# A Trainium2 encoder step: the four plain feed-forward tiles become 2x2 block products, with the norm's factor applied when gate and up are read out

## The chip, the cores and the metric

The kernel runs on one core of one Trainium2 chip. The metric is the device time of one execution in microseconds. The kernel before takes 2283.16 us (median of 3 runs, 2282.57 to 2283.98).

## What is computed

Two layers of an encoder step over 640 tokens (512 prompt, 128 sample) of width 1024, then a final norm. Each layer adds a mixer part (four branches, merged and multiplied with w_out) and then the feed-forward part, which alone the change touches:

```python
def swiglu(h, wg, wu, wd):
    return (jax.nn.silu(h @ wg) * (h @ wu)) @ wd

x = x + swiglu(rmsnorm(x, norm_ffn), w_ff_gate, w_ff_up, w_ff_down)
```

The inner width is 2816, that is 22 tiles of 128. rmsnorm(x, g) multiplies a token's row by one factor (1 over the root of the mean square) and each channel by a gain. The factor is one number per token, so it can also be put on after the product with a weight; but silu needs the scaled gate, and the up product needs the factor too.

## The kernel before, in words

Channels lie on the 128 partitions and tokens along the free axis, so x is 8 tiles of 128x640 f32. A product in full precision is made of three matmuls on a high and a low part: high x high, weight high x activation low, weight low x activation high. High parts are cast by ScalarE (ACT), low parts are a subtraction (value minus high) on GpSimd (POOL) or VectorE (DVE). A matmul moves 320 tokens, half of the 640.

The feed-forward part is written out in FF_FLOW (line 121) as a list of steps, and each engine walks that list in its own order.

- A unit (ff_unit, L1239) is one output tile: for each of its contraction tiles, three matmuls for each half of the tokens. A gate or up unit has 8 contraction tiles, so 48 matmuls.
- A quad (block_product, L1257) is two output tiles at once, as a 2x2 block product with seven products in place of eight (Strassen's scheme in Winograd's form). The blocks are: the two halves of the contraction, the two output tiles, and the two token halves. The seven right operands are named A11, S3, S2, A12, S1, A22, S4; four of the seven weight operands are sums, F_SUM1 to F_SUM4. A gate or up quad is 7 x 4 x 3 = 84 matmuls for a pair of tiles, where units would take 96. A down quad over three pairs of inner tiles is 7 x 3 x 3 = 63 matmuls, and four of them make the 8 output tiles.

Before, pairs 0 and 1 of the 11 pairs (PLAIN = 2, so 4 gate and 4 up tiles) are units, and pairs 2 to 10 are quads. Down goes in four parts: 8 units of 4 tiles (inner tiles 0 to 3), 4 quads over pairs 2 to 4, 4 quads over pairs 5 to 7, and 8 units of 6 tiles (16 to 21).

The units come first for a reason that can be seen in the code: they work on hu_hi and hu_lo, rows with the gain but without the norm's factor (ACT L1731, DVE hu_low L1946), so they can start as soon as the last tile of x is there. While they run, PE sums the squares (L797) and spreads the factor over partitions (L805), ACT and DVE make rstd from it (L1358, L1362, L1928, L1932), gate_out and up_out put the factor on (L2402, L2413), and DVE and ACT prepare the seven operands of the quads with the factor in them (act_block L2422, act_sum L2428, act_high L1756, act_low L2432). From the first quad on no factor is needed.

One gate quad v starts at weight operand number n = v.n. The ring of split weights has RING = 5 slots, so the operand n+5+i can be cast only when product i is done.

- ACT: after product 0 it copies QX to QY (L1788), casts operand n+5 (L1726); after product 1 it copies QW to QZ; after 2 it copies QY to QV and to u2; after 3 it takes silu of QX straight from PSUM (L1791); after 4 it copies QV to u4; then silu of the other three blocks as they come. With each product it casts one more operand. If the quad follows an up quad of a split pair, it casts the blocks of that pair's value (L1809).
- DVE, in this order: three sums of the weights of the next quad (L2380, L2383, L2385), low parts n+5 and n+6 (L2393), the four block sums of the pair before (L2487), the fourth weight sum (L2374), low part n+8, block lows (L2496), the sum QW + u4 (L2468), low part n+9, two block lows, QZ + u2, low part n+11, two block lows. In an up quad there are no follow-ups of a pair before, but four products of gate and up (L2535, L2546, L2558, L2560).
- GpSimd: nothing but low parts (L751). Operands 0 and 3 of a gate or up quad are its own, and 0, 3, 4 and 6 of a down quad (POOL_OPS), in the order of the operands.
- PE: product 2 waits for the first copy, product 4 for the third, product 6 for the fifth; product 0 of the next quad waits until QX is read, product 1 until QW is read. Every product waits for the low part of its weight operand.
- SP loads 512 KB for each half of a quad's weights into four buffers, as soon as the low parts made from that buffer are done.

The main loop that leads into the feed-forward part adds the w_out product to x (L2346), one tile in about 7 us, and for each tile makes the square (ACT L1344), the running sum of squares (add_square, DVE L1961) and hu_hi and hu_lo. The last 8 down units add to x (L2612), sum squares and, in the first layer, make the next layer's operand (ACT L1371, DVE L1951).

## Time and profile before

| what | value |
|---|---|
| median of 3 runs | 2283.16 us |
| lowest and highest run | 2282.57 and 2283.98 us |
| span of the profiled execution | 2280.9 us |
| time around its span (median less span) | 2.3 us |
| PE busy | 2236.0 us, 98%, 14942 matmuls |
| DVE busy | 1425.9 us, 63% |
| ACT busy | 921.1 us, 40% |
| POOL busy | 954.3 us, 42% |
| chain that ended last | PE 87%, DVE 11%, ACT 1% |

The time shown beside the span is that of the runs: the profiled execution's own time is not listed apart, and the span from its first to its last instruction is 2.3 us under the median. The feed-forward part is at 714 to 1144 us in the first layer and again near the end in the second. The mean clock granted to PE over the span is 0.996 of full speed.

### The profile page before, as it was taken

How to read it: one execution, taken by the hardware profiler on the slowest of the kernel's cores; microseconds unless marked ns; L12 is line 12 of the kernel's file. 1: busy time of each engine (PE TensorE's matmuls, PEld its weight loads, DVE VectorE, ACT ScalarE, POOL GpSimd, SP SyncE). 2: the span in 40 equal slices, each digit the busy share in tenths (PEclk: the TensorE clock that was granted, in tenths of full speed). 3: DMA queues.
4: the chain of work that ended last, by engine and by line, in shares of the span. 5: the costliest groups of instructions: out<-in, count | busy, mean ns of one | idle time of the engine just before them, and what ended most of it. 6: DMA issues, size and time to landing. Idle time of an engine off the chain costs nothing.

```text
span 2280.9 us, 40378 instructions
## 1 busy us (share of the span) xinstructions
PE 2236.0 (98%) x14942; PEld 2156.1 (95%) x14942; DVE 1425.9 (63%) x2650; ACT 921.1 (40%) x1886; POOL 954.3 (42%) x988
## 2 busy tenths in 40 slices
PE   8999999999999999999999999999999999999997
PEld 7998998888999999999999999988889999999997
DVE  7998554343235868887489975434432376788864
ACT  4115233445213446665420153334442144566652
POOL 5554454233565433232465444532336644232321
PEclk9999999999999999999999999999999999999998
DMA  5251121011232122222244411210112222222221
GB/s 202 95 181 63 49 73 61 28 42 42 80 106 100 52 96 77 97 81 89 62 139 147 128 54 56 75 51 33 43 42 93 106 93 66 89 89 79 98 79 60
DMA packets 76970, 187.90 MB, mean 82 GB/s; under 512 B 20080, under 2 KB 30928, under 8 KB 75792
## 3 DMA queue, kind: packets, MB, share of 16 engines
q1 hardware_dynamic: 69008, 165.64, 21.9%
q10 hardware_dynamic: 7808, 20.16, 2.6%
q8 instruction: 102, 1.67, 0.3%
q14 instruction: 52, 0.43, 0.1%
HBM read 173.47 MB, written 14.14 MB: 82 GB/s over the span
## 4 chain that ended last, share of the span: by engine, by line
PE 87%; DVE 11%; ACT 1%; issue 1%; DMA 0%; SPq 0%; DVEq 0%; ACTq 0%
PE gemm L778 39%; PE gemm L1257 22%; PE gemm L1239 10%; DVE side L2078 7%; PE side L1257 4%; PE side L1121 2%; PE side L1101 2%; PE side L1052 1%; PE side L884 1%; DVE prod L1987 1%; PE side L1108 1%; DVE h_lo L1941 1%; PE side L972 1%; PE side L1062 1%; PE side L1239 0%
## 5 line engine op out<-in xcount | busy, mean ns | idle before, releaser
L751 POOL TENSOR_TENSOR ring_lo<-w_raw,ring_hi 128x512 fp32r<-128x512 f32 (+2 forms) x232 | 286.0, 1236 | 564.6 <-ACT ring_hi L1726 564.6
L732 POOL CAST w_hi<-w_raw 128x384 fp32r<-128x384 f32 x376 | 223.0, 593 | 702.2 <-PE gemm L778 666.9
L734 POOL TENSOR_TENSOR w_lo<-w_raw,w_hi 128x384 fp32r<-128x384 f32 x376 | 449.7, 1196 | 30.1
L778 PE MATMUL gemm<-h_hi,w_hi 128*128 128x320 f32 x1616 | 406.0, 332 | 6.5 <-DVE h_lo L1941 4.6
L778 PE MATMUL gemm<-h_hi,w_lo 128*128 128x320 f32 x1616 | 368.9, 309 | 0.0
L778 PE MATMUL gemm<-h_lo,w_hi 128*128 128x320 f32 x1616 | 368.3, 309 | 0.0
L778 PEld LDWEIGHTS gemm<-h_hi,w_hi 128*128 128x128 f32 x1616 | 273.8, 189 | 37.9 <-issue 17.1
L778 PEld LDWEIGHTS gemm<-h_lo,w_hi 128*128 128x128 f32 x1616 | 270.6, 188 | 0.0
L778 PEld LDWEIGHTS gemm<-h_hi,w_lo 128*128 128x128 f32 x1616 | 270.4, 188 | 0.0
L1257 PE MATMUL gemm<-act_hi,ring_hi 128*128 128x320 f32 x864 | 267.0, 309 | 0.0
L1257 PE MATMUL gemm<-act_hi,ring_lo 128*128 128x320 f32 x864 | 267.0, 309 | 0.0
L1257 PE MATMUL gemm<-act_lo,ring_hi 128*128 128x320 f32 x864 | 266.9, 309 | 0.0
L1726 ACT ACTIVATE ring_hi<-w_raw 128x512 fp32r<-128x512 f32 (+2 forms) x304 | 172.9, 571 | 122.4 <-PE gemm L1239 65.5
L2078 DVE SCALAR_TENSOR_TENSOR side<-conv_prompt,vec,side 128x512 f32<-128x512 f32 x232 | 175.2, 755 | 0.0
L2173 DVE TENSOR_TENSOR prod<-gate,gemm 128x320 f32<-128x320 f32 x96 | 42.3, 483 | 207.4 <-PE gemm L778 207.4
L1257 PEld LDWEIGHTS gemm<-act_hi,ring_lo 128*128 128x128 f32 x864 | 162.4, 188 | 0.0
L1257 PEld LDWEIGHTS gemm<-act_lo,ring_hi 128*128 128x128 f32 x864 | 162.4, 188 | 0.0
L1257 PEld LDWEIGHTS gemm<-act_hi,ring_hi 128*128 128x128 f32 x864 | 162.3, 188 | 0.0
L778 PE MATMUL gemm<-o_hi,w_hi 128*128 128x320 f32 x512 | 125.5, 326 | 3.1 <-issue 3.1
L778 PE MATMUL gemm<-o_lo,w_hi 128*128 128x320 f32 x512 | 116.8, 309 | 0.0
L778 PE MATMUL gemm<-o_hi,w_lo 128*128 128x320 f32 x512 | 116.7, 309 | 0.0
L2393 DVE TENSOR_TENSOR ring_lo<-w_sum,ring_hi 128x512 fp32r<-128x512 f32 (+1 forms) x156 | 102.7, 659 | 16.7 <-ACT ring_hi L1726 15.5
(357 smaller groups left out, 4703.8 us busy)
## 6 DMA issues: line engine op xcount, KB each, us to landing
w_raw<-in_ws_ff SPq DMA_DIRECT2D x88, 512.0 KB, 3.2
w_raw<-in_ws_gate SPq DMA_DIRECT2D x64, 512.0 KB, 3.2
w_raw<-in_ws_in SPq DMA_DIRECT2D x44, 512.0 KB, 3.3
w_raw<-in_ws_proj SPq DMA_DIRECT2D x64, 256.0 KB, 2.6
w_raw<-in_ws_fq SPq DMA_DIRECT2D x32, 384.0 KB, 3.4
w_raw<-in_ws_out SPq DMA_DIRECT2D x16, 512.0 KB, 3.2
w_raw<-in_ws_fd SPq DMA_DIRECT2D x16, 384.0 KB, 3.0
x_park<-x ACTq DMA_DIRECT2D x2, 2560.0 KB, 13.1
```

The lines of the kernel that those rows point to most:

```text
L732: eng.tensor_copy(w_hi[s][:, cols], w_raw[s][:, cols]).then_inc(w_high.sem, 1)
L734: eng.tensor_tensor(w_lo[s][:, cols], w_raw[s][:, cols], w_hi[s][:, cols].bitcast(F32), ALU.subtract).then_inc(w_split.sem, 1)
L751: eng.tensor_tensor(lo, src, hi.bitcast(F32), ALU.subtract).then_inc(lo_pool.sem, 1)
L778: mm = eng.matmul(dst[:, hf, 0:HALF], w, r[k][:, cols] if r in (xu_hi, xu_lo) else r[:, k, cols], start=first and k == 0 and part == 0, st ...
L1101: eng.matmul(bank[:, 0:w], qh[h % 2][:, P * i:w], kh[h % 2][:, 0:w], start=True, stop=True)\
L1121: mm = eng.matmul(B[6][:, i * P:(i + 1) * P], v_tok[k][:, two], PT[i % 2][:, k * P:(k + 1) * P], start=(k == 0), stop=(k == i))
L1239: mm = eng.matmul(dst[hf], w[:, cut], r[:, cols], start=part == 0 and k == 0 and t == 0, stop=part == 1 and k == tiles - 1 and t == 2)
L1257: mm = eng.matmul(dst, w[:, cut], r, start=fresh and k == 0 and t == 0, stop=k == tiles - 1 and t == 2, skip_group_check=not fresh)
L1726: eng.activation(hi, src, ACT.Copy).then_inc(op_high.sem, 1)
L2078: eng.scalar_tensor_tensor(acc, src, w, acc, ALU.mult, ALU.add).then_inc(conv_step.sem, 1)
L2173: eng.tensor_tensor(t2[0][:, cols], sg[:, cols], G[1][:, hf, 0:HALF], ALU.mult)\
L2393: eng.tensor_tensor(lo, src, hi.bitcast(F32), ALU.subtract).then_inc(lo_dve.sem, 1)
```

## The change

All 11 pairs of gate and up become quads, on rows with the gain but without the factor, and down becomes quads for nine pairs (0 to 8). The last 8 units take 4 tiles (18 to 21). Tables and the order of work:

```diff
-PLAIN = 2
-FF_FLOW = (("gate", 2), ("up", 2), ("units", 0, 4), ("gate", 3), ("up", 3), ("gate", 4), ("up", 4),
-           ("gate", 5), ("downs", (2, 3, 4)), ("up", 5), ("gate", 6), ("up", 6), ("gate", 7), ("up", 7),
-           ("gate", 8), ("downs", (5, 6, 7)), ("up", 8), ("gate", 9), ("up", 9), ("gate", 10), ("up", 10),
-           ("units", 16, 6))
-SPLIT_PAIRS = (2, 3, 4, 5, 6, 7)
+FF_FLOW = (("gate", 0), ("up", 0), ("gate", 1), ("up", 1), ("gate", 2), ("up", 2),
+           ("gate", 3), ("downs", (0, 1, 2)), ("up", 3), ("gate", 4), ("up", 4), ("gate", 5), ("up", 5),
+           ("gate", 6), ("downs", (3, 4, 5)), ("up", 6), ("gate", 7), ("up", 7), ("gate", 8), ("up", 8),
+           ("gate", 9), ("downs", (6, 7, 8)), ("up", 9), ("gate", 10), ("up", 10), ("units", 18, 4))
+SPLIT_PAIRS = tuple(range(9))
```

GpSimd makes the low parts of the first five operands of the first quad, and in every gate quad it multiplies by rstd six times: each of the four gate blocks after silu (value), and the two blocks that are sums before silu (summed):

```diff
+                def quad(v):
+                    gate, pair = v.kind == "gate", v.pair
+                    def value(k, t, cols):
+                        eng.wait_ge(gate_act.sem, gate_act.at(l, 4 * pair + k))
+                        eng.tensor_tensor(gb[t][:, cols], gb[t][:, cols], rstd[:, cols], ALU.mult)\
+                           .then_inc(gate_done.sem, 1)
+                    def summed(k, t):
+                        eng.wait_ge(p_sum.sem, p_sum.at(l, 2 * v.index + k))
+                        eng.tensor_tensor(gb[t][:, hi_half], gb[t][:, hi_half], rstd[:, hi_half], ALU.mult)\
+                           .then_inc(gate_sum.sem, 1)
+                    for i in range(5, 10):
+                        operand_low(v.n + i)
+                    if gate:
+                        value(1, 0, lo_half)
+                        summed(1, 1)
+                        summed(2, 0)
+                    operand_low(v.n + 10)
+                    if gate:
+                        value(2, 1, hi_half)
+                    operand_low(v.n + 11)
+                    if gate:
+                        value(3, 0, hi_half)
+                        value(4, 1, lo_half)
```

DVE multiplies the other two blocks by rstd straight from PSUM:

```diff
+                    done(3)
...
-                    if up:
-                        done(3)
+                    if not up:
+                        eng.tensor_tensor(gb[0][:, lo_half], rstd[:, lo_half], QX, ALU.mult).then_inc(gate_raw.sem, 1)
+                    else:
...
+                    else:
+                        done(6)
+                        eng.tensor_tensor(gb[1][:, lo_half], rstd[:, lo_half], QV, ALU.mult).then_inc(gate_raw.sem, 1)
```

ACT takes silu later, and waits for GpSimd in between; the last two silus of a gate quad go into the next quad, or to the end of the gate quad where a down quad follows:

```diff
-                    if gate:
-                        silu_block(QX, gb[0][:, lo_half])
                     cast(n + 8)
...
                     copied(QV, u4)
+                    if gate:
+                        eng.wait_ge(gate_raw.sem, gate_raw.at(l, 2 * v.pair + 1))
+                        silu_block(gb[0][:, lo_half])
                     cast(n + 9)
...
                     done(5)
+                    cast(n + 10)
                     if gate:
-                        eng.wait_ge(p_sum.sem, p_sum.at(l, 2 * v.index + 1))
-                        silu_block(gb[1][:, hi_half], gb[1][:, hi_half])
+                        eng.wait_ge(gate_sum.sem, gate_sum.at(l, 2 * v.pair + 1))
+                        silu_block(gb[1][:, hi_half])
```

The operands of the quads are now made while the w_out product is added to x, tile by tile, in place of the full hu_hi and hu_lo: for tiles 0 to 3 A11 and S3; for tiles 4 to 7 S1, S2, S4 and A12 (which holds A22 too). The sums of the first quad's weights stand between, and the sum of squares and the factor come in the midst of the first quad:

```diff
+                for m in range(KT):
+                    eng.wait_ge(x_back[m // 4].sem, x_back[m // 4].at(l, 16))
+                    add_to_x(A_UNITS + 2 * M_PAIRS + m, m)
+                    act_sums(l, m)
+                    if m:
+                        add_square(l, 0, m - 1)
+                    for name in (A11, S3) if m < 4 else A_LOWS[:2] if m == 7 else A_LOWS:
+                        act_low(l, m, name)
+                    if m == 6:
+                        weight_sums(FF_QUADS[0], False)
+                weight_sums(FF_QUADS[0], True)
+                add_square(l, 0, KT - 1)
+                for name in A_LOWS[2:]:
+                    act_low(l, KT - 1, name)
+                operand_low(5)
+                operand_low(6)
                 row_factor(l, 1)
```

Here act_sums is one subtraction (S3) for tiles 0 to 3, and for tiles 4 to 7 three operations of 128x320 (S1, S2, S4). On PE, product 0 of the first quad waits for A11 alone, layer_norm_sum stands after product 3 and spread_factor after product 4. The signs of some sums are turned, without another operation. Buffers move, and the weights' bytes stay the same.

## Rows read from the trace of the kernel before

**Rows 1.** The page's part 1, its first line and the engines' busy time.

```profile
span 2280.9 us, 40378 instructions
PE 2236.0 (98%) x14942; PEld 2156.1 (95%) x14942; DVE 1425.9 (63%) x2650; ACT 921.1 (40%) x1886; POOL 954.3 (42%) x988
```

**Rows 2.** The timeline of ACT: copy of QX after product 0 of four quads.

```profile
828.65 0.42 ACT L1788 ACTIVATE gemm<-gemm 128x320 f32<-128x320 f32 x1 [1.13 <-PE gemm L1257]
...
853.29 0.42 ACT L1788 ACTIVATE gemm<-gemm 128x320 f32<-128x320 f32 x1 [1.08 <-PE gemm L1257]
...
865.61 0.42 ACT L1788 ACTIVATE gemm<-gemm 128x320 f32<-128x320 f32 x1 [0.44 <-PE gemm L1257]
```

**Rows 3.** Windows: gate with follow-ups, up, down quad: PE, PEld, DVE, ACT, POOL busy.

```profile
851.50:863.83 12.33, 12.33 (x86) 12.33 (x86) 11.79 (x21) 8.43 (x19) 2.57 (x3) 1.00 0.26 87
863.83:876.14 12.31, 12.31 (x86) 12.31 (x86) 9.33 (x17) 7.45 (x16) 2.94 (x3) 1.00 0.21 65
885.40:894.70 9.30, 9.30 (x65) 9.30 (x65) 8.68 (x15) 6.33 (x16) 4.16 (x4) 1.00 0.15 44
```

**Rows 4.** Timeline of GpSimd, low parts of three widths.

```profile
833.53 1.30 POOL L751 TENSOR_TENSOR ring_lo<-w_raw,ring_hi 128x512 fp32r<-128x512 f32 x1 [5.92 <-ACT ring_hi L1726]
...
882.71 1.02 POOL L751 TENSOR_TENSOR ring_lo<-w_raw,ring_hi 128x384 fp32r<-128x384 f32 x1 [6.24 <-ACT ring_hi L1726]
...
1101.95 0.74 POOL L751 TENSOR_TENSOR ring_lo<-w_raw,ring_hi 128x256 fp32r<-128x256 f32 x1 [1.95 <-ACT ring_hi L1726]
```

**Rows 5.** Timelines of GpSimd and DVE around 858 us.

```profile
858.17 1.57 POOL L751 TENSOR_TENSOR ring_lo<-w_raw,ring_hi 128x512 fp32r<-128x512 f32 x1 [6.34 <-ACT ring_hi L1726]
...
858.10 0.49 DVE L2487 TENSOR_TENSOR f_block<-square,f_block 128x320 f32<-128x320 f32 x1
858.51 1.79 DVE L2374 TENSOR_TENSOR w_sum<-w_raw,w_sum 128x512 f32<-128x512 f32 x1
...
869.88 0.68 DVE L2374 TENSOR_TENSOR w_sum<-w_raw,w_sum 128x512 f32<-128x512 f32 x1
```

**Rows 6.** The same timelines around 863 us, and DVE's idle time after it.

```profile
863.17 1.33 POOL L751 TENSOR_TENSOR ring_lo<-w_raw,ring_hi 128x512 fp32r<-128x512 f32 x1 [3.42 <-ACT ring_hi L1726]
...
863.26 0.48 DVE L2468 TENSOR_TENSOR gate<-side,square 128x320 f32<-128x320 f32 x1
865.20 0.69 DVE L2393 TENSOR_TENSOR ring_lo<-w_raw,ring_hi 128x512 fp32r<-128x512 f32 x1 [1.45 <-ACT ring_hi L1726]
```

**Rows 7.** DVE's timeline in the up quad that began at 863.83: low part 5, product.

```profile
868.67 0.68 DVE L2393 TENSOR_TENSOR ring_lo<-w_sum,ring_hi 128x512 fp32r<-128x512 f32 x1
...
870.89 0.49 DVE L2535 TENSOR_TENSOR prod<-gate,gemm 128x320 f32<-128x320 f32 x1 [0.33 <-PE gemm L1257]
```

**Rows 8.** DVE's timeline at the last tile of x and the factor.

```profile
714.82 0.89 DVE L2346 TENSOR_TENSOR x<-gemm,x 128x320 f32<-128x320 f32 x2 [4.62 <-PE gemm L778]
...
716.41 0.82 DVE L1961 TENSOR_TENSOR gate<-gate,square 128x640 f32<-128x640 f32 x1
...
718.03 1.92 DVE L1961 TENSOR_TENSOR gate<-gate,square 128x640 f32<-128x640 f32 x1
723.15 0.19 DVE L1928 RECIPROCAL rstd_tokens<-rstd_tokens 128x5 f32<-128x5 f32 x1 [3.19 <-ACT rstd_tokens L1358]
723.37 0.90 DVE L1932 TENSOR_TENSOR prod<-ident,rstd_tokens 128x384 f32<-128x384 f32 x2
```

**Rows 9.** Timelines where the last units begin: PE, ACT, DVE.

```profile
1097.73 0.46 PE L1239 MATMUL side<-f_hi,ring_hi 128*128 128x320 f32 x2
...
1099.15 0.72 ACT L1752 ACTIVATE hu_hi<-square 128x640 fp32r<-128x640 f32 x1
...
1099.27 1.40 DVE L2418 TENSOR_TENSOR hu_lo<-prod,hu_hi 128x640 fp32r<-128x640 f32 x1 [0.85 <-ACT hu_hi L1752]
1100.60 0.81 DVE L2418 TENSOR_TENSOR hu_lo<-square,hu_hi 128x640 fp32r<-128x640 f32 x1
...
1119.86 1.88 DVE L1961 TENSOR_TENSOR gate<-gate,square 128x640 f32<-128x640 f32 x1
```

More of the change, by code:

```diff
@@ L173, in unit @@
         units.append(len(ops))
-        first = min(4, (tiles + 1) // 2) if tiles < 6 else 4
+        first = tiles // 2
         add(len(loads) - 1, 0, first * P, True)
@@ L183, in quad @@
                                                    (a, HW, F_SUM1), (a + 1, 0, F_SUM4), (a + 1, HW, None))):
-            add(load, start, cols, i in POOL_OPS[q.kind], summed, q)
-    for _ in range(4 * PLAIN):
-        unit(KT)
+            add(load, start, cols, i in by_pool, summed, q)
     q = d = 0
-    last, units_since = None, len(units)
+    last = None
     for step in FF_FLOW:
@@ L201, in _ff_operands @@
                 unit(step[2])
-            units_since = len(units)
         for v in new:
-            v.g, v.before, v.units = len(quads), last, units_since
-            if last is not None and not units_since:
+            v.g, v.before = len(quads), last
+            if last is not None:
                 last.after = v
-            last, units_since = v, 0
+            last = v
             quad(v)
@@ L2368, in split_before @@
                     def split_before(k):
-                        eng.wait_ge(lo_dve.sem, lo_dve.at(l, FF_OPS[v.before.n + k].count if v.before else 0))
+                        if v.before and not FF_OPS[v.before.n + k].pool:
+                            eng.wait_ge(lo_dve.sem, lo_dve.at(l, FF_OPS[v.before.n + k].count))
                     if fourth:
@@ L2511, in quad @@
                     split = up and pair in SPLIT_PAIRS
[L2512 removed]
+                    follows = b is not None and b.kind == "up" and b.pair in SPLIT_PAIRS
                     def done(i):
```

485 lines of the change are left out of this document (224 added, 261 removed).

## The prediction

> **What bounds the kernel now.** I read the page first: PE is busy 2236.0 of 2280.9 us [rows 1], so what is taken from PE is worth its time, as long as nothing else becomes late. Then PE's waits: inside the quads there are none, and the feed-forward part has almost none. So the trace holds no stall that the change could remove; it can only shorten PE's work. Then the windows of one quad each. A gate quad with follow-ups lasts 12.33 us and DVE is busy 11.79 us of it; an up quad has 9.33 of 12.31; a down quad 8.68 of 9.30 [rows 3]. DVE stands close behind PE. Its spare time over a pair is 24.64 - 21.12 = 3.5 us. ACT (15.9 us in a pair) and GpSimd (5.5) have room. Last, the timelines of DVE and GpSimd side by side, since the change gives GpSimd new work.
>
> **PE's work.** Quads start 12.32 us apart (853.29 to 865.61, and 24.64 us for two from 828.65) [rows 2], which is 12.32 / 84 = 0.1467 us a matmul. Four gate and up pairs of tiles a layer turn from 96 matmuls into 84: 48 fewer. Down was 8 x 24 + 8 x 63 + 8 x 36 = 984 matmuls and is 12 x 63 + 8 x 24 = 948: 36 fewer. That is 84 a layer, 168 in all, 168 x 0.1467 = **24.6 us saved**. The bytes of weights are the same.
>
> **DVE's own work.** Two multiplications from PSUM in each gate quad, 0.48 us each as its like in [rows 6], so DVE's pair goes from 21.1 to 22.1 us of 24.64. The spare time shrinks to 2.5 us. Removed with the units are gate_out, up_out, act_block and act_low, all beside PE.
>
> **GpSimd's work and what it does to DVE.** GpSimd gets six multiplications of 128x320 with both inputs in SBUF in each gate quad. The trace has no such instruction. Low parts take 0.74, 1.02 and 1.30 us for 256, 384 and 512 columns [rows 4]; between the first two, 320 columns are 0.88 us. Bounds: 0.74 below and 1.02 above. GpSimd's pair becomes 5.5 + 5.3 = 10.8 us, still under half.
>
> The price is on DVE. At 858 us a low part on GpSimd ran for 1.57 us in place of 1.30, as DVE had begun a sum just before it, and DVE's next sum, two inputs in SBUF, took 1.79 us where the same one alone takes 0.68 [rows 5]: it ended 0.56 us after GpSimd did. At 863 us DVE read PSUM beside the same GpSimd instruction and took its usual 0.48 [rows 6]. So the two exclude each other when DVE has both inputs in SBUF, about 1.1 us for 512 columns and, by width, 0.7 to 0.75 for 320. Now GpSimd's low parts mostly fall where DVE waits or reads PSUM, and DVE's quads have room for that.
>
> I lay a pair out from the start of the gate quad, with DVE's order of the trace. The QX multiplication comes at 8.7, ACT's silu at 9.6 (after the copy to u4), GpSimd's value 1 at 10.1. DVE's QW sum is there at 10.6; summed 1 runs to 12.2 and holds up low part n+9 or the block lows by 0.7. The QZ sum comes at 13.4, so summed 2 at 13.6 to 14.3; it blocks n+11 by 0.45. Behind it stand low part n+10, which fell on DVE's idle 1.45 us before [rows 6] and now blocks it for 1.15, then value 2, 3, 4. DVE has from here nothing but sums and low parts with two SBUF inputs until 19 us, so each of the three blocks it by 0.73, and as DVE is late the next quad's low part 7 falls in too, 1.15. In all 0.25 + 0.7 + 0.45 + 1.15 + 3 x 0.73 + 1.15 and 0.4 for the up quad's own n+10 = 6.3 us of blocking a pair. DVE would need 22.1 + 6.3 = 28.4 us where PE needs 24.64. That is 3.8 us a pair by which DVE sets the pace.
>
> Where PE first feels it: low part n+5 of the up quad was ready at 868.67 + 0.68 - 863.83 = 5.5 us into the quad [rows 7] and is needed at 5 x 1.76 = 8.8. It has 3.3 us to spare and would come 4.6 later in a first pair, 7 later in the next: stalls of 1.3, then some 3.6 for each pair.
>
> The other end is given by the down quads: there GpSimd is busy 4.16 us and DVE 8.68, of which by my count of its 15 instructions about 6.6 is its own work; half of GpSimd's time blocks. With half of 5.3 a pair needs 22.1 + 2.65 = 24.8 us, PE's 24.64: no stall to speak of. This is the low bound (0.1 a pair) against 3.8. I take 2.9 for a pair, nearer the layout, since in it GpSimd's operations follow right on DVE's results and fall into its densest stretch.
>
> A gate quad before a down quad is dearer: a down quad's product takes 1.32 us, so its operands are due sooner, four low parts are GpSimd's, and values 2 to 4 stand between them. Bounds 1 and 4.5 us; I take 3.5. DVE enters about 1.8 us late at no cost, once for each run of quads between two relaxed stretches. A layer has three such runs, each of two pairs and one gate quad before down: 2 x 2.9 + 3.5 - 1.8 = 7.5 us (bounds 1 and 10). Pair 0 has no follow-ups in its gate quad but begins late: 1.5. Pair 10 has none either: 0. Sum a layer 3 x 7.5 + 1.5 = 24.
>
> The Trainium skill's page "SBUF — State Buffer", section "Who interferes with whom", says that a DVE instruction with two SBUF inputs and a GpSimd instruction that reads SBUF block each other fully, whoever issues first, and one with at most one SBUF input doesn't. By that rule every GpSimd operation in the dense stretch costs DVE its whole length, and the sum would be the layout's 3.8 a pair, not the half that the down quads show. Rows 5 and 6 agree with it (1.79 against 0.68 and 0.48 us).
>
> **The start of the feed-forward part.** Before, DVE had 4.62 us idle ahead of the last tile of x [rows 8] and PE went on at once with units. Now for tiles 4 to 7 DVE does the addition (0.8), three sums (1.5), squares (0.8), four low parts (2.0): 5.1 us of 7.04 and at tile 6 three weight sums (2.1) more, with GpSimd's five low parts (1.3 each) of the first operands falling in the same place. So it comes to the last tile 1 to 2 us late. S2 of tile 7 is due 3.5 + 1.3 = 4.8 us after the last unit; the chain is addition, ACT's gained half 0.4, S1, S2, S4 1.5, squares 0.8 (1.92 if blocked [rows 8]), low part 0.4: 4.0, plus lateness 1 to 2, plus up to two blockings of 1.1. Behind it stand A12, the fourth sum, the squares that layer_norm_sum needs, S1, S4, two operand low parts, then reciprocal and spreading (1.1 [rows 8]) before spread_factor after product 4. Lower bound 1.5, upper 6; I take 3.5 a layer.
>
> **The end.** In the last units tiles 20 and 21 now come 1.76 us after the start, not 3.52. Units began at 1097.73, the low part of tile 20 was done at 1100.67 [rows 9], so PE waits 1.2 us, bounds 0.7 and 2. Units take 3.52 us in place of 5.28; DVE's addition, squares and next operand are 0.81 + 0.73 + 0.8 = 2.4, with one blocking as at 1119.86 (1.88 us) [rows 9] 3.5. It just fits; 0 to 1 us in the first layer. I take 1.5 a layer together.
>
> **Sum.** -24.6 + 2 x (24 + 3.5 + 1.5) = -24.6 + 58 = +33 us on the span of 2280.9, so 2314 with 2.3 us around it; it stands on the median in the same way, 2283.2 + 33 = 2316. I round the terms down once for the doubt in the blocked share and give **2312 us**.
>
> **Rivals.** A difference of 0.2%, 4.6 us, is about what a measurement of this kernel can tell from none.
>
> 1. *DVE and GpSimd take turns, DVE sets the pace* (the forecast, other side of rival 2): 2290 to 2350. For: rows 3 and 5. The point from which it decides: blocking over 2.5 us a pair. Chance 0.52.
> 2. *The blocking is hidden as in the down quads.* Pairs stall 0 to 0.7 us, start and end cost 5 a layer, gates before down 1.5: -24.6 + 10 + 9 = -6, 2277; if the start fits too, -24.6 + 8 = -17, 2266. For: GpSimd is half idle and half of its time was free before. Against: DVE's 11.79 of 12.33. Chance 0.33, of it 0.26 under 2278.6.
> 3. *ACT waits in line for GpSimd.* gate_sum holds ACT until summed 1 is done, and behind it stand the cast n+11 and the copy of QX for the next quad, which product 2 needs at 15.8. If GpSimd's operations are 1.0 us or more, the copy comes 1 to 2 us late in each of 22 gate quads: +33, less 24.6, with start and end 2301. Against: about 1.5 us of slack in the layout. Chance 0.12.
> 4. *The change doesn't do what it says*, fewer matmuls gained than 168: 0.03.
>
> Faster 0.27, same 0.08, slower 0.65. The range, 2266 to 2346, leaves out the upper bound of all terms and the best of rival 2.
>
> **What would show it.** PE x14774, its busy time hardly smaller as waits appear at L1257 with DVE L2393 (ring_lo) as releaser, 1 to 4 us each, above all in the fifth product of up quads and the first of down quads. DVE's windows of a pair near 27 to 28 us and full; sums (L2380, L2383, L2374) with means well over 0.68. GpSimd's multiplication at 0.9 to 1.6 us. DVE's share in the chain of waits above 11%. Wrong if windows of a pair stay at 24.64 and PE waits only at the start; then the blocking was hidden. If the releaser is ACT's copy, rival 3.

## The result, and the profile after

The changed kernel takes 2328.44 us (median of 4 runs, 2327.0 to 2329.11) against 2283.19 (2282.57 to 2283.98) of the kernel before: ratio 1.0193, 95% interval 1.0179 to 1.0208. It is slower by 45 us, as forecast in sign and cause (2312, range 2266 to 2346), and 16 us slower than the forecast.

First the page, its span, busy times and the shares of the chain of waits:

```profile
span 2326.5 us, 40875 instructions
PE 2231.4 (96%) x14774; PEld 2137.5 (92%) x14774; DVE 1633.7 (70%) x2888; ACT 989.9 (43%) x2078; POOL 1093.9 (47%) x1110
...
PE 62%; DVE 32%; issue 4%; ACT 2%; DVEq 0%; POOL 0%; DMA 0%; SPq 0%; ACTq 0%
```

Against [rows 1] PE has its 168 matmuls less, but only 4.6 us less busy time; DVE is busy 208 us longer for 238 instructions more, which is 0.87 us for each: too much for two multiplications of 0.48 and some low parts. So DVE's old instructions have become longer. DVE's share of the chain is 32%.

PE's waits (engine, line, what it waited for: sum in us, times, longest) name the place:

```profile
PE side L1320 <- DVE ring_lo L2482: 32.0, 23, 2.5
PE gemm L1320 <- ACT gemm L1798: 8.5, 8, 1.4
...
PE gemm L1320 <- issue: 3.7, 2, 1.8
```

Inside the quads the kernel before had no such wait. The releaser of most is DVE's low part of a weight operand. ("issue" is time for which the view finds no releaser.) The pace of a run is read, as in [rows 2], from ACT's copy of QX, here of gate 2, gate 3 and the first down quad behind it:

```profile
778.90 0.42 ACT L1798 ACTIVATE gemm<-gemm 128x320 f32<-128x320 f32 x1 [1.08 <-PE gemm L1320]
...
806.77 0.42 ACT L1798 ACTIVATE gemm<-gemm 128x320 f32<-128x320 f32 x1 [1.08 <-PE gemm L1320]
...
821.07 0.42 ACT L1798 ACTIVATE gemm<-gemm 128x320 f32<-128x320 f32 x1
```

A pair takes 27.87 us where PE needs 24.64. The windows of the gate and the up quad of pair 2 (columns as in [rows 3]) show DVE full:

```profile
777.11:790.18 13.07, 12.85 (x87) 12.58 (x87) 12.83 (x22) 8.55 (x18) 3.34 (x4) 1.00 0.25 80
790.18:804.98 14.80, 12.31 (x85) 12.05 (x84) 14.63 (x19) 8.02 (x17) 9.54 (x8) 1.00 0.18 54
```

DVE is busy 27.46 of 27.87 us; without GpSimd's multiplications it is 22.07 (run 3 below), so 5.4 us of a pair are blocking, where the prediction's layout had 6.3. The timelines of DVE and GpSimd in pair 1 show what fills it (start, duration):

```profile
764.62 1.19 DVE L2482 TENSOR_TENSOR ring_lo<-w_raw,ring_hi 128x512 fp32r<-128x512 f32 x1
765.74 2.67 DVE L2539 TENSOR_TENSOR f_block_lo<-f_block,f_block_hi 128x320 fp32r<-128x320 f32 x2
768.33 1.36 DVE L2469 TENSOR_TENSOR w_sum<-w_raw,w_raw 128x512 f32<-128x512 f32 x1
769.73 1.25 DVE L2472 TENSOR_TENSOR w_sum<-w_sum,w_raw 128x512 f32<-128x512 f32 x1
771.02 1.64 DVE L2474 TENSOR_TENSOR w_raw<-w_raw 128x512 f32<-128x512 f32 x1
...
764.38 0.88 POOL L787 TENSOR_TENSOR gate<-gate,rstd 128x320 f32<-128x320 f32 x1 [1.23 <-DVE gate L2511]
765.22 1.75 POOL L773 TENSOR_TENSOR ring_lo<-w_raw,ring_hi 128x512 fp32r<-128x512 f32 x1
766.93 1.13 POOL L782 TENSOR_TENSOR prod<-prod,rstd 128x320 f32<-128x320 f32 x1
768.02 1.12 POOL L782 TENSOR_TENSOR gate<-gate,rstd 128x320 f32<-128x320 f32 x1
769.11 1.33 POOL L782 TENSOR_TENSOR prod<-prod,rstd 128x320 f32<-128x320 f32 x1
770.39 1.71 POOL L773 TENSOR_TENSOR ring_lo<-w_raw,ring_hi 128x512 fp32r<-128x512 f32 x1
```

GpSimd has no gap for 7.7 us, and each of DVE's instructions takes about twice its time (a sum of 512 columns 0.68 alone [rows 5], here 1.25 to 1.64): the two take turns here, instruction by instruction, as at 858 us in [rows 5]. That happens where the prediction's layout put it, from the sum QW + u4 to the next quad's low part 7. The multiplication alone takes 0.88 us, as estimated from the widths of [rows 4].

In a gate quad before a down quad a second wait shows, on ACT (in brackets: idle time before, and who ended it) and then on PE:

```profile
820.33 0.47 ACT L1838 ACTIVATE gate<-gate 128x320 f32<-128x320 f32 x1 [1.22 <-POOL gate L787]
...
821.53 0.41 PE L1320 MATMUL gemm<-f_block_hi,ring_hi 128*128 128x320 f32 x1 [1.43 <-ACT gemm L1798]
```

This is rival 3, in this one place only: ACT stands in line for GpSimd's "summed 2", and the copy of QX for the next quad behind it comes late (at 821.07, shown above).

The start of the feed-forward part has four gaps on PE, and DVE, which had 4.62 us idle before the last tile of x [rows 8], now comes to it without a gap, at 718.61 us. PE's last w_out matmul ended at 715.64 (714.71 before), so DVE is 3.0 us behind it where it was 0.1:

```profile
716.49 0.41 PE L1320 MATMUL gemm<-hu_hi,ring_hi 128*128 128x320 f32 x1 [0.70 <-POOL ring_lo L773]
...
721.18 0.41 PE L1320 MATMUL gemm<-s_hi,ring_hi 128*128 128x320 f32 x1 [0.90 <-ACT gemm L1798]
...
723.80 0.42 PE L1320 MATMUL gemm<-s_hi,ring_hi 128*128 128x320 f32 x1 [1.03 <-DVE s_lo L2043]
...
729.10 0.39 PE L1320 MATMUL gemm<-s_hi,ring_hi 128*128 128x320 f32 x1 [1.83 <-issue]
...
717.02 1.67 DVE L2474 TENSOR_TENSOR w_raw<-w_raw 128x512 f32<-128x512 f32 x1
718.61 0.88 DVE L2443 TENSOR_TENSOR x<-gemm,x 128x320 f32<-128x320 f32 x2
...
724.46 0.68 DVE L2463 TENSOR_TENSOR w_sum<-w_raw,first_sum 128x512 f32<-128x512 f32 x1
...
727.20 0.68 DVE L2482 TENSOR_TENSOR ring_lo<-w_raw,ring_hi 128x512 fp32r<-128x512 f32 x1
...
728.37 2.48 DVE L1993 TENSOR_TENSOR prod<-ident,rstd_tokens 128x384 f32<-128x384 f32 x2
...
724.47 6.10 POOL L773 TENSOR_TENSOR ring_lo<-w_raw,ring_hi 128x512 fp32r<-128x512 f32 x2 [3.39 <-ACT ring_hi L1793]
```

The diagonals for the factor took 0.90 before [rows 8], 2.48 now beside GpSimd's low parts. PE's largest gap, the 1.83 of "issue", stands ahead of product 4 and so ahead of the spreading; the diagonals end at 730.85, after PE goes on. What ends 0.1 us before PE goes on is the first of GpSimd's two low parts, that of operand 4: it runs from 724.47 to 729.00, 4.53 us where 1.30 is usual. From 724.46 to 727.88 DVE runs six instructions with two SBUF inputs one right behind the other, each in its usual time (0.68 for a sum), and GpSimd ends 1.1 us after the last. So here it was GpSimd that was held up, and not in turns. The same 6.1 us for the two low parts stand at the second layer's start and in run 3. When the two alternate and when one is held for several instructions, no run here shows.

The granted clock stays at 1.00 through this start, but not through the same start of the second layer: it has the same four gaps, and the windows of 4 us from 1872 and 1876 show 0.84 and 0.73. Quad 0 lasts 18.37 us there, against 17.41 in the first layer.

The last units start with one gap of 0.39 us, and the next layer's sum of squares in layer 0 follows with another. The rows are PE's sum of squares in the timeline of the kernel before, the same in the changed one, and the changed kernel's windows around it:

```profile
1143.84 1.25 PE L797 MATMUL side<-ones,gate 128*128 128x1 f32 x10 [0.17 <-issue]
```

```profile
1166.58 1.25 PE L860 MATMUL side<-ones,gate 128*128 128x1 f32 x10 [1.30 <-issue]
```

```profile
1164.00:1168.00 4.00, 2.70 (x21) 2.47 (x20) 3.74 (x3) 1.73 (x4) 3.84 (x4) 1.00 0.99 390
1168.00:1172.00 4.00, 4.00 (x19) 4.00 (x18) 1.61 (x3) 0.22 (x1) 2.35 (x3) 0.57 0.78 302
```

After PE's wait the granted clock is 0.57 for 4 us (for the most part the 1.2 GHz level), 19 matmuls where there would be 29: some 1.5 to 1.7 us beside the 1.1 of the longer wait.

### The profile page after: what moved, and what is told of

Its sections match the earlier page's. It is cut to its first block, busy times and chain, and to the rows that moved or that the text cites. A ratio compares the mean times of both kernels' runs of the same rounds, so it can differ in the third digit from the quotient of the medians.

```text
span 2326.5 us, 40875 instructions
## 1 busy us (share of the span) xinstructions
PE 2231.4 (96%) x14774; PEld 2137.5 (92%) x14774; DVE 1633.7 (70%) x2888; ACT 989.9 (43%) x2078; POOL 1093.9 (47%) x1110
## 3 DMA queue, kind: packets, MB, share of 16 engines
q8 instruction: 101, 1.65, 0.3%
## 4 chain that ended last, share of the span: by engine, by line
PE 62%; DVE 32%; issue 4%; ACT 2%; DVEq 0%; POOL 0%; DMA 0%; SPq 0%; ACTq 0%
PE gemm L841 36%; PE gemm L1320 10%; DVE side L2175 7%; DVE ring_lo L2482 5%; DVE f_block_lo L2539 4%; PE gemm L1302 2%; PE side L1320 2%; DVE w_raw L2474 2%; DVE w_sum L2472 2%; PE side L1184 2%; DVE w_sum L2469 2%; DVE f_block L2530 2%; PE side L1164 1%; DVE w_sum L2463 1%; PE side L1115 1%
## 5 line engine op out<-in xcount | busy, mean ns | idle before, releaser
L773 POOL TENSOR_TENSOR ring_lo<-w_raw,ring_hi 128x384 fp32r<-128x384 f32 (+2 forms) x218 | 279.3, 1283 | 382.9 <-ACT ring_hi L1793 382.6
L1320 PE MATMUL gemm<-s_hi,ring_hi 128*128 128x320 f32 x696 | 217.3, 312 | 9.3 <-issue 3.7
L1320 PE MATMUL gemm<-s_hi,ring_lo 128*128 128x320 f32 x696 | 215.7, 310 | 0.0
L1320 PE MATMUL gemm<-s_lo,ring_hi 128*128 128x320 f32 x696 | 215.6, 310 | 0.0
L1320 PEld LDWEIGHTS gemm<-s_hi,ring_hi 128*128 128x128 f32 x696 | 131.2, 189 | 12.7 <-ACT square L1798 4.0
L1320 PE MATMUL gemm<-f_block_hi,ring_hi 128*128 128x320 f32 x432 | 134.8, 312 | 6.7 <-ACT gemm L1798 6.7
L1793 ACT ACTIVATE ring_hi<-w_sum 128x512 fp32r<-128x512 f32 (+1 forms) x200 | 117.2, 586 | 39.5 <-PE gemm L1320 20.9
L1320 PE MATMUL gemm<-f_block_lo,ring_hi 128*128 128x320 f32 x432 | 133.6, 309 | 0.0
L1320 PE MATMUL gemm<-f_block_hi,ring_lo 128*128 128x320 f32 x432 | 133.5, 309 | 0.0
L1320 PEld LDWEIGHTS gemm<-s_hi,ring_lo 128*128 128x128 f32 x696 | 131.5, 189 | 0.0
```

The lines of the kernel that those rows point to most:

```text
L773: eng.tensor_tensor(lo, src, hi.bitcast(F32), ALU.subtract).then_inc(lo_pool.sem, 1)
L1320: mm = eng.matmul(dst, w[:, cut], r, start=fresh and k == 0 and t == 0, stop=k == tiles - 1 and t == 2, skip_group_check=not fresh)
L1793: eng.activation(hi, src, ACT.Copy).then_inc(op_high.sem, 1)
```

## The experiments

All are timed against the kernel before on the same chip. Where part of the computation is left out or replaced, it is said.

**1. No second factor.** The four GpSimd multiplications behind the silu are left out (the second factor is not applied); the waits stay.

```diff
-                        eng.tensor_tensor(gb[t][:, cols], gb[t][:, cols], rstd[:, cols], ALU.mult)\
-                           .then_inc(gate_done.sem, 1)
+                        eng.sem_inc(gate_done.sem, 1)
```

> The changed kernel without GpSimd's four multiplications of the gate blocks by the norm's factor after silu (88 a layer pair of gate quads in all, 4 in each of 22); the second factor is left out of the result, the two multiplications of sums before silu stay. Theory A (a GpSimd instruction that reads SBUF and a DVE instruction with two SBUF inputs exclude each other, and DVE sets the pace): the two pairs in a row fall from 27.9 us to 24.7 to 25.2, and of the some 53 us of stalls in the quads some 43 go: 2285 us, between 2280 and 2295. Theory B (ACT waits in line for GpSimd's two multiplications before silu): these stay, so at most 10 us are gained: 2318 or more. Theory C (the loss is in the start of the feed-forward part, the pairs only pass it on): 2323 or more.

Measured: 2291.60 us, ratio 1.0031 (1.0021 to 1.0042). This is in the expected range. 36.8 us of the loss go, and PE's waits for DVE's low parts fall from 32.0 to 6.3 us. Pairs in the middle of a run take 24.64 us again. What is left is mostly in the gate quads before down, 13.65 to 14.01 us against 11.88 in run 3, where PE still waits 1.0 to 1.1 us for ACT's copy, which stands behind GpSimd's "summed 2".

**2. The same four as memset.** In place of each multiplication a memset of the same 128x320 (the gate's value is 0.5).

```diff
-                        eng.tensor_tensor(gb[t][:, cols], gb[t][:, cols], rstd[:, cols], ALU.mult)\
-                           .then_inc(gate_done.sem, 1)
+                        eng.memset(gb[t][:, cols], 0.5).then_inc(gate_done.sem, 1)
```

> The changed kernel with each of the four multiplications after silu replaced by a memset of the same 128x320 block to 0.5 on GpSimd, which reads nothing; the gate's value is left out of the result. Theory A: GpSimd is as busy in kind, but reads nothing from SBUF, so DVE is not blocked: within 5 us of the run without the multiplications, 2285 to 2290. Theory D (it is GpSimd's queue that is late, its low part n+10 behind three other instructions): the time stays above 2305 if a memset takes near 0.9 us, and lies in proportion if it is shorter.

Measured: 2291.22, ratio 1.0029 (1.0017 to 1.0041), the same as without them. An instruction on GpSimd in the same place of its queue, which reads nothing, costs nothing. It is shorter, though (0.37 us against 0.88), so this alone does not part "reads" from "long"; run 5 helps, but no run has an instruction that only writes and lasts 0.88 us.

**3. No factor on GpSimd at all.** All six multiplications are left out (on the two summed blocks the factor is missing altogether, on the others the second one).

```diff
-                        eng.tensor_tensor(gb[t][:, hi_half], gb[t][:, hi_half], rstd[:, hi_half], ALU.mult)\
-                           .then_inc(gate_sum.sem, 1)
+                        eng.sem_inc(gate_sum.sem, 1)
```

> The changed kernel without any multiplication on GpSimd, so without the second factor and without the first one on the two blocks that are sums. After the run without the four (2291.6 us), Theory A gives another 2 x 0.7 us of blocking a pair, where only gate quads before down and the later pairs of a run still stall: 2281 to 2288. If the rest of the loss is in the start, 2289 or more.

Measured: 2273.16 (2272.58 to 2273.96), ratio 0.9949 (0.9932 to 0.9965): a miss on the good side. I had priced the two multiplications at 4 to 11 us after the 2291.6 of run 1 and put the rest on the start; they cost 18.4. The windows of pair 2's two quads:

```profile
772.18:784.50 12.32, 12.32 (x86) 12.32 (x86) 11.91 (x22) 8.46 (x19) 1.91 (x2) 1.00 0.27 85
784.50:796.82 12.32, 12.32 (x86) 12.32 (x86) 10.16 (x19) 7.49 (x16) 3.56 (x3) 1.00 0.21 65
```

PE is without a gap again and DVE has 22.07 us of work in a pair, which is the prediction's 22.1. The same group of DVE's instructions between 740 and 820 us, first in the changed kernel, then here (busy us, mean ns):

```profile
L2539 DVE TENSOR_TENSOR f_block_lo<-f_block,f_block_hi 128x320 fp32r<-128x320 f32 x11 | 11.0, 1038 | 0.0
```

```profile
L2537 DVE TENSOR_TENSOR f_block_lo<-f_block,f_block_hi 128x320 fp32r<-128x320 f32 x12 | 6.4, 573 | 0.0
```

So the six multiplications cost 2328.44 - 2273.16 = 55.3 us, 132 of them at 0.42 us each. Taken out in this order, the four and the two have the same price: 36.8 / 88 and 18.4 / 44 are both 0.42. The ways are not the same: with the four, DVE's blocked low parts make PE wait; of the 18.4 us of the two, 5.9 are PE's idle time for ACT's copies in the six gate quads before down (rival 3), which is gone in run 3.

**4. Neither GpSimd's nor DVE's.** As 3, and DVE's two multiplications from PSUM are left out too; silu reads PSUM (no factor is applied to the gate).

```diff
-                        eng.tensor_tensor(gb[0][:, lo_half], rstd[:, lo_half], QX, ALU.mult).then_inc(gate_raw.sem, 1)
+                        eng.sem_inc(gate_raw.sem, 1)
...
-                        silu_block(gb[0][:, lo_half])
+                        silu_block(gb[0][:, lo_half], QX)
```

> The same, and DVE's two multiplications of a gate quad left out too: silu reads PSUM, as before. The factor is left out of the result entirely, while all work to make it stays. What is left of the change is its block products, the new start and the short last units: 2283.2 - 24.6 + the start. With the start at 8 us a layer as the trace of the changed kernel has it, 2275; with nothing but it the quads run at 12.32 us each and the gate quads before down at most 0.5 us over. 2270 to 2279.

Measured: 2272.91, ratio 0.9945 (0.9928 to 0.9961), run 3 within its spread. DVE's part of the change costs nothing. The kernel before took 2284.7 beside these runs, so what separates both from 2284.7 - 24.6 = 2260 is the start and the end: 13 us.

**5. The kernel before, with six idle multiplications.** In the kernel before, GpSimd gets six products of 128x320 in each of the 18 gate quads of pairs 2 to 10, from one SBUF tile into a scratch tile, three before and three after its own low part of the next quad's operand 3 (the three before are shown). Nobody waits for them. Then the same with memset.

```diff
+                    if here and n == q.n + 3:
+                        for k in (1, 1, 1):
+                            eng.wait_ge(gate_act.sem, gate_act.at(l, 4 * (pair - PLAIN) + k))
+                            extra(k)
```

> The kernel before, with six instructions more on GpSimd in the wake of each of its 18 gate quads, three ahead of the next quad's low part 3 and three behind it: a product of two halves of a table in SBUF, 128x320, written to an unused tile. Nobody waits for them but GpSimd itself; the result is the same. Theory A: they block DVE by 0.73 us each wherever it has two SBUF inputs, and low part n+10 moves onto DVE's dense stretch: a pair needs 21.1 + 4.5 to 6 us on DVE for 24.64 on PE, so it is slower by 1 to 2.5 us a pair after the first of a run, with the gate quads before down: 2300 to 2325. Theory B (order and latency of the factor on ACT and DVE): nothing waits here, so 2283 to 2288.

> The same, with a memset of the unused tile (0.37 us in the run with memsets) in place of each product, which reads nothing. Theory A: within 0.1% of the kernel before, 2282 to 2286. Theory D (GpSimd's own queue is late): a third to a half of what the run with products loses.

Measured: 2310.42 with the products, ratio 1.0108 (1.0091 to 1.0125); 2283.94 with memset, ratio 0.9998 (0.9989 to 1.0008). GpSimd's own groups of the two, between 700 and 1150 us:

```profile
L754 POOL TENSOR_TENSOR scratch<-cos_sin 128x320 f32<-128x320 f32 x54 | 57.8, 1070 | 5.4 <-ACT gate L1811 0.5
```

```profile
L754 POOL MEMSET scratch<- 128x320 f32 x54 | 19.8, 367 | 4.7 <-ACT gate L1811 0.6
```

Both are as expected. This is the cleanest of the runs: nothing waits for the products and PE's and DVE's work is unchanged. Work that no one needs costs 26.5 us, 0.25 each for 108. One line is left, GpSimd's own: its low parts stand behind three products. PE notices that in four places, ahead of product 3 of the first down quad behind gates 5 and 8 of each layer, with 0.97 to 0.99 us each: at 899.42 us it goes on 0.1 us after a low part that GpSimd began only when its three products were done (at 898.02). These are some 4 of the 26.5 us. With 19.8 us of memset in a layer nothing moves; were it GpSimd's busy time that costs, these would have cost 26.5 x 19.8 / 57.8 = 9 us. By the Trainium skill, page "SBUF — State Buffer", section "Who interferes with whom", a DVE instruction with two SBUF inputs contends with a GpSimd instruction that reads SBUF and not with one that only writes. The two runs agree with it.

**6. All six on DVE.** DVE multiplies while it reads PSUM: the two sums of the gate, and in the up quad the up block by the factor, ahead of gate times up.

```diff
-                    summed(QZ, u2, QZ if up else gb[0][:, hi_half])
+                    summed(QZ, u2, QZ)
+                    if not up:
+                        gate_scaled(2, QZ, 0)
...
+                        scaled_up(3, QZ, hi_half)
```

> The changed kernel with all six multiplications by the factor moved from GpSimd to DVE, each with its input in PSUM (the up product's block is multiplied in PSUM in place of the gate's after silu; the result is the same). Theory A: DVE's own pair grows from 22.1 to 25.0 us by six instructions of 0.48 us, and blocking falls from 6.3 to 0.5 to 1.2: a pair takes 25.5 to 26.3 us in place of 27.9, and the kernel 2300 to 2310. If DVE's count of instructions and not the blocking set the pace (Theory E), a pair would be 27.9 + 2.9 and the kernel 2360 or more.

Measured: 2322.22 (2320.34 to 2324.43), ratio 1.0164 (1.0147 to 1.0181), a miss (2300 to 2310 expected): only 6 us better than the changed kernel. Windows of pair 2's quads, then the timeline of DVE, ACT and PE in the gate quad:

```profile
775.77:789.92 14.15, 12.86 (x86) 12.33 (x86) 13.88 (x26) 8.77 (x19) 2.53 (x3) 1.00 0.23 75
789.92:802.62 12.70, 12.59 (x86) 12.33 (x86) 12.49 (x22) 7.52 (x16) 3.25 (x3) 1.00 0.21 64
```

```profile
782.77 1.78 DVE L2473 TENSOR_TENSOR ring_lo<-w_sum,ring_hi 128x512 fp32r<-128x512 f32 x1
...
785.59 1.92 ACT L1854 ACTIVATE f_block_hi<-f_block 128x320 fp32r<-128x320 f32 x4 [2.07 <-DVE f_block L2521]
787.42 0.42 ACT L1789 ACTIVATE square<-gemm 128x320 f32<-128x320 f32 x1
...
787.89 0.42 PE L1311 MATMUL gemm<-s_hi,ring_hi 128*128 128x320 f32 x1 [1.25 <-ACT square L1789]
```

DVE's sum is 22.07 + 2 x 0.48 + 4 x 0.49 = 25.0 us by its own work and was measured as 26.37, and the pair takes 26.85 us where I expected 25.5 to 26.3. At 25.0 DVE is already over PE's 24.64, and as it is now late it also meets GpSimd's own low parts (1.78 above where 0.68 is usual). PE notices it through ACT, which stands waiting for DVE's block sums with the copy behind it. The larger part of the miss lies in the gate quads before down, for which the expectation had no term: by the copies of QX they take 15.9 us against 11.88 in run 3, 12 of the 24 us that a layer loses between up 0 and up 9. Taking the work from the shared turns to the full engine saved 6 us of 55.

**7. The factor folded into x, first form.** Pairs 0 to 8 go without the second factor, and x is divided by it instead (8 multiplications of 128x640 by DVE, in gate 0 and up 0), then multiplied back in up 9 and gate 10. The two summed blocks stay with GpSimd.

```diff
+                        eng.reciprocal(t2b[:, :], rstd[:, :]).then_inc(std_made.sem, 1)
...
+                        for k in range(4):
+                            x_times(k, t2b[:, :])
```

> The second factor is taken out of pairs 0 to 8: x is divided by the norm's factor (a reciprocal of 128x640 and 8 multiplications of 128x640 by DVE in gate 0 and up 0), down adds to it, and 8 multiplications in up 9 and gate 10 bring it back; pairs 9 and 10 keep GpSimd's multiplications. The result is the same. Theory A: GpSimd is left with two multiplications in a gate quad, so the quads cost as in the run without the four, and the 16 multiplications of 0.8 us lie in the quads where DVE has 3 to 4 us to spare: 2286 to 2296. Rival: they do not fit into pair 0, which starts late, and add 3 to 5 us a layer: 2296 to 2305.

Measured: 2317.45, ratio 1.0143 (1.0127 to 1.016), a miss, and beyond the rival's 2296 to 2305 as well. DVE's timeline and the window behind it:

```profile
737.53 4.14 DVE L2630 RECIPROCAL prod<-rstd 128x640 f32<-128x640 f32 x1
741.71 7.08 DVE L2571 TENSOR_TENSOR x<-x,prod 128x640 f32<-128x640 f32 x8
```

```profile
748.00:760.00 12.00, 8.50 (x39) 8.50 (x40) 10.13 (x20) 3.80 (x8) 1.28 (x1) 0.60 0.14 44
```

A reciprocal of 640 columns takes 4.14 us, nearly five times a product of that size (7.08 / 8), and with the block of eight it holds DVE for 11.2 us. PE waits up to 7.7 us and then works at a granted clock of 0.60. Up 0 takes 22.99 us by the copies of QX and 12.32 in run 1: 10.7 a layer, so 21 of the 26 us by which this run is over run 1. Runs 9 and 10 try the same multiplications in other places.

**8. First operand earlier.** The changed kernel, with the high part of the first weight operand cast one x tile earlier.

```diff
-                    if k == 6:
-                        for n in range(RING - 1):
+                    if k == 5:
+                        cast(0)
+                    elif k == 6:
+                        for n in range(1, RING - 1):
```

> The changed kernel, with the high part of operand 0 of the first product made by ACT one x tile earlier, so that GpSimd makes its low part beside another stretch of DVE's sum of squares. It asks how much of the start, some 8 us a layer more than before, is one first operand that comes late. Theory A (the first operands wait in one line behind DVE and GpSimd's shared turns; only the first of them moves): 1 to 3 us a layer less than the changed kernel, 2323 to 2327 us. Rival (the start is set by DVE's chain of the last x add, the scalings of the first activation blocks and their parts, which this does not touch): 2327 to 2330 us, no difference that can be measured. Had the first operand been all of it: 2313 us or less.

Measured: 2326.26 (2325.38 to 2329.19), ratio 1.0187 (1.0173 to 1.0201). The gap of 0.70 is gone from the trace, the other three stay (0.94, 1.01, 1.83). The median is 2 us lower, but the intervals of the two ratios overlap: the size is not shown by the times, only the gap by the trace. The profiled execution is the slowest of the five: behind these gaps its granted clock is 0.50 in the window of 4 us from 728, and quad 0 takes 19.59 us. The start is not one late operand. The gap of 0.70 and that of 1.83 wait for two different low parts of GpSimd (operands 0 and 4), and only the first was moved; the other two wait for ACT's copy and for DVE's low part of S2.

**9 and 10. The factor folded, second form.** No factor work on GpSimd. The summed blocks as in 6; the second factor goes into x for pairs 0 to 8, by an inverse spread by PE from a 128x5 column, the 8 multiplications strewn over the quads up 0 to gate 3; 10 has the earlier first operand too.

```diff
+UP_TILES = {1: (0,), 2: (1,), 3: (2, 3), 4: (4,), 5: (5, 6), 6: (7,)}
...
+                    if up:
+                        for k in UP_TILES.get(v.g, ()):
+                            x_down(k)
```

> A version that keeps the block products of all pairs, but takes the factor off GpSimd altogether. The first factor on the two summed blocks of a gate is multiplied by DVE while it reads them from PSUM; the second factor is not applied for pairs 0 to 8 but x is divided by it instead (x holds x over the factor from up 0 to up 6's downs, 8 multiplications of 128x640 by DVE spread over the up quads 1 to 6), and multiplied back in up 9 and gate 10; the spread of the inverse factor is made by PE from a 128x5 column, not by a reciprocal of 128x640, whose 4.14 us were in the run before. Pairs 9 and 10 have the second factor by DVE. Theory A (what the change lost was GpSimd's shared turns with DVE, as the runs without the second factor showed with 2273 us; what is added costs 0.9 us for each of 16 x multiplications where DVE has no slack, nothing where it has): 2275 to 2285 us, near or under the kernel before. Rival (DVE's two longer multiplications from PSUM hold up ACT's copies and so PE, as in the run with all six on DVE, whose pairs took 26.9 us in place of 24.64): half or more of that stays, 2290 to 2310 us.

> The version of the run before (the factor folded into x), with the earlier first operand as well. Theory A: the same 1 to 3 us a layer below that run, so 2270 to 2282 us; if the first operand is covered by DVE's own chain at the start, the same time as that run within 1 us.

Measured: 2308.37 and 2307.04, ratios 1.0110 (1.0094 to 1.0125) and 1.0101 (1.0085 to 1.0116). 20 us better than the changed kernel, 24 to 25 worse than the one before: misses for Theory A of both, and the rival of run 9. The difference between the two, 1.3 us, is not clear of the noise. By the copies of QX, the run up 0 to the first down quad takes 82.6 us (73.5 in run 3), the runs two and three 76.4 each. Those two have no x multiplication, so 2.9 us each are the price of two multiplications of 0.48 us on each gate quad's sums: nine such microseconds in a layer, where I had put nothing. In the run from up 3 on, the next quads keep PE's pace (four take 49.2 us, with DVE busy 98% of gate 4 to gate 5), and 2.6 of the 2.9 us fall in the gate quad before down, 14.46 us against 11.88. It is the place of rival 3 again, with DVE where GpSimd was:

```profile
931.38 0.47 ACT L1842 ACTIVATE gate<-gate 128x320 f32<-128x320 f32 x1 [2.57 <-DVE gate L2584]
...
932.63 0.42 PE L1317 MATMUL gemm<-f_block_hi,ring_hi 128*128 128x320 f32 x1 [1.79 <-ACT gemm L1802]
```

ACT waits for DVE's multiplication of the QZ sum (L2584), and the copy of QX stands behind its silu.

**11. ACT's order.** Version 10, with ACT's copy of product 4 ahead of the four block roundings that wait for DVE.

```diff
-                    if follows:
-                        for name in (S3, S1, S2, S4):
-                            block_high_made(b.pair, name)
                     done(4)
                     copied(QV, u4)
+                    if follows:
+                        for name in (S3, S1, S2, S4):
+                            block_high_made(b.pair, name)
```

> The version with the folded factor and the earlier first operand, with one change of order on ACT: in a quad that follows a blocked up, the copy of product 4 comes before the high parts of the four block sums, which wait for DVE, and not behind them. In the run before, PE waited 9.5 us a layer for ACT's copies, most of it in the gate quads that follow a blocked up. Theory A (DVE is only just full there; what PE waits for is ACT's place in line behind DVE's sums): most of these waits go, 4 to 8 us a layer, so 2291 to 2299 us. Rival (DVE itself is over its time in these quads, 24.6 us a pair, and the wait only comes back as one for the next low parts): within 2 us of the run before, 2305 to 2309 us.

Measured: 2312.42 (2308.65 to 2313.8), ratio 1.0119 (1.0102 to 1.0136): no gain, and outside both expected ranges; 5 us over version 10, but the intervals of the two ratios overlap. PE's waits in the first feed-forward part, of version 10 and of this one:

```profile
PE gemm L1317 <- ACT gemm L1802: 7.3, 4, 2.8
PE side L1317 <- DVE ring_lo L2488: 2.3, 2, 1.5
...
PE gemm L1317 <- ACT square L1802: 2.2, 2, 1.3
```

```profile
PE gemm L1317 <- ACT gemm L1802: 8.5, 4, 3.5
PE side L1317 <- DVE ring_lo L2488: 5.0, 5, 2.1
```

The wait for that copy (square) is gone, 2.2 us, and 2.7 more stand at DVE's low parts. The order decided who is late there, not that someone is. The larger wait, 7.3 us, is for another copy, mostly that of QX ahead of the down quads, and this edit does not touch it. None of these versions beats the kernel before; runs 3 and 4, 10 us under it, leave the factor's work out.

## Why the prediction was right, point by point

- **PE's saving.** x14774 as said, and in run 3 the quads are back at 12.32 us: 24.6 us are there to be had. In the changed kernel PE's idle time grows from 44.9 to 95.1 us, and its busy time falls by 4.6 and not by 24.6. Run 3 has the same matmuls in 2217.0 us of busy time, so 14 us of the loss stand inside the busy time of the changed kernel. A lower granted clock is part of that (0.57 for 4 us above); the rest was not separated.
- **DVE's own work.** 22.1 us a pair, free: shown by runs 3 and 4.
- **The blocking.** The forecast's mechanism is shown by runs 1 to 3 and 5. The layout said DVE needs 28.4 us a pair, I took 2.9 us of stall between 0.1 and 3.8, measured are 27.87 - 24.64 = 3.23. The layout was nearer than the half that I had read off the down quads. The rule of the Trainium skill's page "SBUF — State Buffer", section "Who interferes with whom", which the prediction weighed against that half, would have given 3.8 there. The layout was a little high in the blocking itself, 6.3 against 5.4.
- **Gate before down.** Taken 3.5. From gate 3's copy to the first down quad's 14.30 us, against 11.88 in run 3, so 2.4, and the down quads behind it, for which the prediction had no term, lose 1.3 more (38.69 against 37.41): 3.7.
- **The runs together.** From up 0 to up 9 the changed kernel takes 359.7 us and run 3 332.7: 27.0 a layer, in both layers. The prediction had 24. By parts it had 9.0, 7.5 and 7.5 for the three runs, and they lose 9.5, 6.9 and 6.9; the down quads make up the rest. That the sum comes so near is partly luck, since a gate quad before down was taken too dear and the down quads at nothing.
- **The start** was mis-sized: "Lower bound 1.5, upper 6; I take 3.5 a layer". Quad 0, from its copy of QX to the next one's, lasts 17.41 us and not 12.32, 5.1 more, and the first gap stands ahead of it: 5.8. In the second layer, where the clock falls, it lasts 18.37: 6.8 in all. The chain was right up to S2 of the last x tile, and DVE came 2.9 us late to that tile where I had said 1 to 2: I had counted DVE's own work there and added only two blockings at the end, none for the weight sums, of which two took 1.65 and 1.67 us. What followed was not in the sum: the largest gap, 1.83, is not the factor's but that of operand 4, whose low part on GpSimd I had at 1.3 us and which took 4.53 behind DVE's instructions.
- **The end.** Taken 1.5 a layer. The first gap is 0.39 and not 1.2, but in layer 0 the next norm's sum waits 1.1 us longer, and the clock costs 1.7: 3.6 for both layers, against 3. The fall of the clock was in no term.
- **The sum.** 2 x 27.0 + 5.8 + 6.8 + 3.6 = 70.2 of loss, less 24.6, is 45.6, as the spans differ. The prediction's own sum was 58 - 24.6 = 33. Rounding it down "for the doubt in the blocked share" was wrong in direction; of the 12 us between the losses, 6 are the runs, between 5 and 6 the start and under 1 the end.
- **The rivals.** Rival 2 (hidden as in the down quads) falls with the pace of a pair. Rival 3 is real in one place, the gate quad before down, where PE's wait for ACT's copy (1.24 to 1.43 us) is the larger part of the 2.1 to 2.4 us; in all it is 6.7 us of idle time in six quads. With the value multiplications gone PE's waits for ACT's copies hardly shrink (8.5 to 7.7 us), while DVE's fall from 32.0 to 6.3, so it does not set the time of the pairs. Rival 4: the count of matmuls refutes it.

## What to carry to other kernels

GpSimd is not a free engine beside a busy DVE: an instruction of it that reads SBUF takes its time from DVE's instructions with two SBUF inputs. Where DVE's own work was nine tenths of PE's time (22.1 of 24.6 us), about half of it landed on the path (0.42 us of each 0.88); at 21.1 of 24.6 it was 0.25. The other way round, a long row of such DVE instructions can hold up GpSimd, as the 4.53 us of one low part show. Before work is given to GpSimd, add it to DVE's window of the bounding stage, not to GpSimd's; the same six multiplications on DVE itself cost 49 us in place of 55, so the question is the window and not the engine. Look at the quad whose successor is shortest as well: in every version timed with the whole factor in it, PE waited for ACT's copy of QX behind the gate quad before down. To test such a suspicion, put the suspected instruction into the old kernel with nobody waiting for it, and beside it one of another kind.

## What the runs showed that I had not expected

- The price of a GpSimd multiplication came out the same in both groups (0.42 us for the four, 0.42 for the two of a gate quad), though they reach PE on different ways; in the kernel before it was 0.25.
- A memset of 128x320 on GpSimd takes 0.37 us and cost DVE nothing (ratio 0.9998), where a product of the same size takes 0.88 alone and 1.07 in the mean.
- A reciprocal of 128x640 on DVE takes 4.14 us, 6.5 ns a column; the same over 128x5 takes 0.19 [rows 8].
- The granted clock fell to 0.57 for 4 us after a gap of 1.3 us ahead of a short norm sum, which cost more than the gap. The four gaps of 0.7 to 1.8 us at the start of the feed-forward part left it at 1.00 in the first layer of the changed kernel's trace and were followed by 0.84 and 0.73 in the second, and by 0.50 in the first layer of run 8's profile, which has three of them. So the same gaps can cost nothing or a microsecond or two from one pass to the next. What decides was not tried.
- A low part on GpSimd took 4.53 us in place of 1.30 while DVE ran six instructions with two SBUF inputs in their usual times: the one that is held up need not be DVE.
- Two multiplications of 0.48 us from PSUM in each gate quad cost 2.9 us in each run of six quads (runs 9 and 10), while two others of the same size cost nothing (run 4): with the one pair DVE is at 22.1 us of 24.64 and nothing is late; with both, the quads in the middle of a run still keep PE's pace, and the gate quad before down does not.
